# Reordering the opening of a two-block transformer kernel: activations first, query from unshifted activations

## What is computed

```
mod = silu(c) @ w_ada + b_ada                 # 1024 x 6144: shift, scale, gate, twice
sh1, sc1, gt1, sh2, sc2, gt2 = split(mod, 6)
h = rmsnorm(x, g_mix) * (1 + sc1) + sh1       # per token norm, per feature scale and shift
proj = h @ w_in                               # q, k, v, o, gates, u
q = q * 128 ** -0.5
# gates -> log_sigmoid, cumulative sums and maxima over the tokens -> decay of an mLSTM,
# in both directions, four heads of 128; then pooling, output projection, feed forward, a second block
```

## Time and profile before

| | us |
|---|---|
| median of 3 runs | 1655.7 |
| lowest, highest | 1654.61, 1656.57 |
| the profiled execution, its own time | 1656.27 |
| its span, first to last instruction | 1654.5 |
| PE busy | 1631.2 (99% of the span) |
| DVE busy | 1072.2 (65%) |
| ACT busy | 737.4 (45%) |
| POOL busy | 237.6 (14%) |
| DMA | 199.3 MB, 120 GB/s over the span |

### The profile page before, as it was taken

One profiled execution on the slowest core, in us unless ns is written; L12 is line 12 of the kernel. 1 busy time (PEld: TensorE's weight loads), 2 busy tenths in 40 slices (PEclk: granted clock), 3 DMA queues, 4 the chain that ended last, 5 costly groups with the idle time before them and its releaser, 6 DMA issues.

```text
span 1654.5 us, 20244 instructions
## 1 busy us (share of the span) xinstructions
PE 1631.2 (99%) x7833; PEld 1308.0 (79%) x7833; DVE 1072.2 (65%) x1358; ACT 737.4 (45%) x971; POOL 237.6 (14%) x255
## 2 busy tenths in 40 slices
PE   6999999999999999999999999999999999999999
PEld 3887778888898887887666788886688888888887
DVE  2897778543575577786766855548768876642464
ACT  3543334322374235646775433538822464431242
POOL 0014300050220000001766000004600000000000
PEclk9999999999999999999999999999999999999999
DMA  9556423222222232225664222220032222222223
GB/s 378 197 205 255 161 77 102 89 90 102 103 102 102 88 142 81 103 76 202 211 221 156 77 102 74 100 98 27 2 128 96 83 102 103 99 82 100 102 102 102
DMA packets 31151, 199.30 MB, mean 120 GB/s; under 512 B 3504, under 2 KB 4008, under 8 KB 10832
## 3 DMA queue, kind: packets, MB, share of 16 engines
q1 hardware_dynamic: 27168, 171.63, 28.9%
q10 hardware_dynamic: 3888, 26.38, 4.0%
HBM read 193.60 MB, written 4.40 MB: 120 GB/s over the span
## 4 chain that ended last, share of the span: by engine, by line
PE 90%; DVE 6%; ACT 2%; DMA 1%; issue 1%; POOL 0%; SPq 0%; DVEq 0%; ACTq 0%; POOLq 0%
PE bank1to L1869 14%; PE bank1to L1871 14%; PE bank1to L1870 14%; PE bank L1869 13%; PE bank L1870 12%; PE bank L1871 12%; PE bank L2319 2%; PE bank1to L2435 2%; PE bank L2447 1%; PE bank L2461 1%; DVE w_lo L1016 1%; DMA x<-x_in 1%; DVE ada_sum L1152 1%; PE bank L2153 1%; PE bank L1977 1%
## 5 line engine op out<-in xcount | busy, mean ns | idle before, releaser
L477 ACT ACTIVATE w_hi<-raw 128x2048 fp32r<-128x2048 f32 (+1 forms) x133 | 247.4, 1860 | 312.9 <-DMA raw<-slabs 300.2
L1016 DVE TENSOR_TENSOR w_lo<-raw,w_hi 128x2048 fp32r<-128x2048 f32 (+1 forms) x125 | 291.6, 2333 | 100.3 <-ACT w_hi L477 96.8
L1869 PE MATMUL bank<-h,w_hi 128*128 128x512 f32 (+1 forms) x736 | 290.5, 395 | 0.9 <-ACT qa L477 0.7
L1870 PE MATMUL bank<-h,w_hi 128*128 128x512 f32 (+1 forms) x736 | 285.9, 388 | 0.0
L1871 PE MATMUL bank<-h,w_lo 128*128 128x512 f32 (+1 forms) x736 | 285.6, 388 | 0.0
L1869 PEld LDWEIGHTS bank<-h,w_hi 128*128 128x128 f32 x736 | 138.2, 188 | 35.5 <-issue 7.8
L1871 PEld LDWEIGHTS bank<-h,w_lo 128*128 128x128 f32 x736 | 138.2, 188 | 28.9
L1870 PEld LDWEIGHTS bank<-h,w_hi 128*128 128x128 f32 x736 | 138.3, 188 | 27.9 <-issue 1.0
L1869 PE MATMUL bank1to<-h,w_hi 128*128 128x512 f32 (+1 forms) x416 | 159.7, 384 | 0.0
L1871 PE MATMUL bank1to<-h,w_lo 128*128 128x512 f32 (+1 forms) x416 | 159.3, 383 | 0.0
L1870 PE MATMUL bank1to<-h,w_hi 128*128 128x512 f32 (+1 forms) x416 | 159.3, 383 | 0.0
(11 more groups left out here) (519 smaller groups left out, 2746.1 us busy)
## 6 DMA issues: line engine op xcount, KB each, us to landing
raw<-slabs SPq DMA_DIRECT2D x127, 1024.0 KB, 4.8
ada_chunk<-ada ACTq DMA_DIRECT2D x24, 1024.0 KB, 8.1
p<-sum_rows SPq DMA_DIRECT2D x32, 640.0 KB, 5.5
x<-x_in SPq DMA_DIRECT2D x4, 1024.0 KB, 8.5
p<-decay_rows SPq DMA_DIRECT2D x6, 640.0 KB, 7.4
spill_x<-x SPq DMA_DIRECT2D x1, 2048.0 KB, 10.8
x<-spill_x SPq DMA_DIRECT2D x2, 1024.0 KB, 5.9
out<-x SPq DMA_DIRECT2D x8, 256.0 KB, 2.0
```

The costliest lines, as they stand in the source:

```text
L477: return act.activation(out, in_, f, **kw)
L1016: do.tell(dve.tensor_tensor(w_lo[:, n % SLOTS, part], raw[:, n % SLOTS, part], w_hi[:, n % SLOTS, part].bitcast(f32), ALU.subtract), "w_sp ...
L1869: pe.matmul(out, w[0], a[0], start=start, stop=False)
L1870: pe.matmul(out, w[0], a[1], start=False, stop=False)
```

## The change

- SP issues `cols`, the first half of `x`, `consts`, chunk pair 2, slab 0, then chunk pairs 3 to 7, `gw`, slab 1; slab 2 waits for chunk pair 7 (before: for chunk 6). ACT issues the second half of `x` and chunk pairs 0 and 1. A chunk pair is two blocks of 128 features by 1024 columns: pairs 0 to 3 hold the scale, 4 to 7 the shift.
- The norm's sum: ACT squares into a ring of four buffers, DVE adds the eight squares (seven additions), PE sums over the features with four matmuls of one column, ACT takes the root of 128x4, DVE inverts it, PE spreads it (`spread`) into bank 6, and DVE multiplies the tiles of `x` with it in place, four ahead of slab 0's tail and four in the loop.
- q_0 is computed from `x * gain` without the shift. Chunk pairs 4 to 7 are multiplied between its tiles, the shift's row is turned, and the shifted `h` is made in a second pass (DVE `tensor_scalar`, ACT rounded head, DVE tail). The gate product runs on it alone, with the product of the shift and q_0's weights (32 matmuls of two columns, `shift_product`) between its tiles; ACT adds that bias to q_0 as it empties the banks.
- The split of the gate weights moves from DVE to POOL. Fillers change in number and place. Several semaphores are merged under one name.

```diff
@@ sync
-            for k in range(0, KT, 4):
-                sp.dma_start(x[:, k:k + 4, :], x_d[:, k:k + 4, :]).then_inc(sem("x_in"), 16)
+            sp.dma_start(x[:, 0:4, :], x_d[:, 0:4, :]).then_inc(sem("x_in"), 16)
             sp.dma_start(consts[:], consts_d).then_inc(sem("consts_in"), 16)
-            sp.dma_start(gw[:], gate_w_d).then_inc(sem("consts_in"), 16)
+            first_ada(2)
...
                 if n == 1:
-                    sp.wait_ge(sem("ada_in6"), 16)
+                    for part in range(3, KT):
+                        first_ada(part)
+                    sp.dma_start(gw[:], gate_w_d).then_inc(sem("gate_w_in"), 16)
+                if n == 2:
+                    sp.wait_ge(sem("ada_in7"), 16)
@@ scalar
+            for k in range(KT):
+                if k >= 4:
+                    act.wait_ge(sem("sq_used"), max(1, k - 4))
+                do.tell(fn(squares_ring[k % 4], x[:, k, :], ACT.Square), "sq_ready", k + 1)
+            act.wait_ge(sem("first_total"), 2)
+            do.tell(fn(first_root, banks[7][:, 0:TOK], ACT.Sqrt, bias=eps), "root_ready", n_root)
             weight_head(0)
             mod_copy(0, banks[4])
+            for k in range(KT):
+                act.wait_ge(sem("h_scaled"), max(4, k + 1))
+                do.tell(fn(h_hi[:, k, :], x[:, k, :], ACT.Copy, scale=gain[:, k:k + 1]), "unshifted_head", k + 1)
+            weight_head(1)
+            mod_copy(1, banks[5])
+            act.wait_ge(sem("shift_split"), 1)
+            for k in range(KT):
+                ...
+                do.tell(fn(h_hi[:, k, :], x[:, k, :], ACT.Identity, scale=gain[:, k:k + 1], bias=mod[:, SH1 + k:SH1 + k + 1]),
+                        "h_head", k + 1)
             ada_refill(KT, KT + 2)
+            weight_head(2)
+            act.wait_ge(sem("shift_taken"), 1)
+            for t in range(2):
+                tile_ready("q_0", t)
+                free(fn(qk[:, t, :], banks[t][:], ACT.Identity, scale=DH ** -0.5, bias=shift_bias[:, t:t + 1]), "q_0", t)
+            act.wait_ge(sem("h_ready"), KT)
             ada_refill(KT + 2, KT + 4)
             act.wait_ge(sem("gates_done"), 1)
@@ vector
+            for k in range(4):
+                do(dve.tensor_tensor(x[:, k, :], x[:, k, :], root_bank[:], ALU.mult))
             weight_tail(0)
+            first_mod(0, SC1, banks[4])
+            ...
+            for k in range(KT):
+                if k < 4:
+                    do.tell(dve.tensor_tensor(x[:, k + 4, :], x[:, k + 4, :], root_bank[:], ALU.mult), "h_scaled", k + 5)
+                dve.wait_ge(sem("unshifted_head"), k + 1)
+                do.tell(dve.scalar_tensor_tensor(h_lo[:, k, :], ...), "unshifted_ready", k + 1)
+            weight_tail(1)
+            first_mod(1, SH1, banks[5])
+            ...
+            shifted(0)
+            for k in range(KT):
+                if k + 1 < KT:
+                    shifted(k + 1)
+                dve.wait_ge(sem("h_head"), k + 1)
+                do.tell(dve.tensor_tensor(h_lo[:, k, :], (t0, t1)[k % 2][:], ...), "h_ready", k + 1)
+            dve.wait_ge(sem("shift_done"), 1)
+            ...
+            weight_tail(2)
             do(dve.memset(row_parts[:].bitcast(f32), 0.0))
-            for n in range(1, 3):
-                weight_tail(n)
@@ tensor
+            mod_chunk(0)
+            kept_busy(banks[3], 12)
+            pe.wait_ge(sem("first_total"), 1)
+            for t in range(TOK):
+                last = pe.matmul(banks[7][:, t:t + 1], rs[:, P * t:P * t + P], mean[:, 0:1], start=True, stop=True)
+            last.then_inc(sem("first_total"), 1)
+            mod_chunk(1)
+            kept_busy(banks[3], 5)
+            pe.wait_ge(sem("consts_in"), 16)
+            pe.wait_ge(sem("first_total"), 3)
+            spread(first_root, "first_total")
+            mod_chunk(2)
+            kept_busy(banks[3], 8)
+            mod_chunk(3)
+            kept_busy(banks[3], 2)
             mod_turn(0, banks[4])
+            kept_busy(banks[3], 16)
             pe.wait_ge(sem("w_split"), 1)
             for k in range(KT):
+                pe.wait_ge(sem("unshifted_ready"), k + 1)
                 ...
+                for n in {2: (4, 5), 4: (6,), 5: (7,)}.get(k, ()):
+                    mod_chunk(n)
+                if k == 6:
+                    mod_turn(1, banks[5])
+            pe.wait_ge(sem("gate_w_split"), 1)
+            for k in range(KT):
+                shift_product(k, SLAB0["q_0"], banks[7], 1)
+                pe.wait_ge(sem("h_ready"), k + 1)
+                gates = three(banks[5][:], (gw_hi[:, k, :], gw_lo[:, k, :]), (h_hi[:, k, :], h_lo[:, k, :]), k == 0, k == KT - 1)
+            gates.then_inc(sem("gates_done"), 1)
```

More of the change, by code:

```diff
@@ L574, in root_copy @@
                 do.tell(fn(rs[:], root_bank[:], ACT.Copy), "root_copied", n)
-            def norm():
-                squares([x[:, k, :] for k in range(KT)], sq)
-                root(rs)
             def heads(stage, shift=None, place=h_hi, between=None):
@@ new lines, in _ @@
+            for k in range(2, KT):
+                dve.wait_ge(sem("sq_ready"), k + 1)
+                ins = dve.tensor_tensor(total, total, squares_ring[k % 4], ALU.add)
+                if k < KT - 1:
+                    do.tell(ins, "sq_used", k)
+                else:
+                    do.tell(ins, "first_total", 1)
+            n_root = 1
+            dve.wait_ge(sem("root_ready"), n_root)
+            do.tell(dve.reciprocal(first_root, first_root), "first_total", 3)
+            dve.wait_ge(sem("first_total"), 4)
@@ L1219, in _ @@
+            do.tell(dve.tensor_scalar(shift_bias[:], shift_bias[:], DH ** -0.5, None, ALU.mult), "shift_taken", 1)
+            weight_tail(2)
             do(dve.memset(row_parts[:].bitcast(f32), 0.0))
-            for n in range(1, 3):
-                weight_tail(n)
             do(dve.tensor_scalar(half_gain[:], cols[:, COLS["g_head"]:COLS["g_head"] + H1], 0.5, None, ALU.mult))
@@ L1864, in _ @@
         def _(pe):
-            n_sq = 0
             def three(out, w, a, start, stop):
```

248 lines of the change are left out of this document (119 added, 129 removed).

## The result

The changed kernel is slower: a median of 1660.0 us (15 runs, 1657.7 to 1663.8) against 1655.2 (15 runs, 1654.3 to 1657.4), a ratio of 1.0030 with a 95% interval from 1.0022 to 1.0038. Forecast were 1656.0 us and a range up to 1659.5. Even among the rest single executions differ by more than the effect of some parts, so both kernels were profiled twice.

The account below looks back on a forecast made before the run. PE was taken as the bound, busy 1631.2 of 1654.5 us. Of 9.8 us won at the product 9.5 go by k_0; decay work 2.55 later puts `weighted` at +0.3: 1655.7 + 0.3 = 1656.0, range 1651.5 to 1659.5 (8 in 10).

Parts of the forecast that it names:

- the sum from the first product to the transposes of the decay rows: PE from product at 31.3 to k_0 at 57.2, then 28.0 us plus 0.5 waiting for q_1's tail: transposes at 85.8.
- Up to the product: Opening: column total at 18.5 us, held 2.1 by fillers; first product at 31.3 against 41.14, 9.8 won.
- From the product to k_0: PE's chunks, turn and second pass between product and k_0: 9.5 of 9.8 us given back, k_0 at 57.2 against 57.55.
- the step that decides: Decay work after late gate rows: DVE starts at 60.8 against 58.25, 2.55 later; `weighted` at 92.75 against 92.45, +0.3 us.
- From here both lists are as before: Behind `weighted`: the lists stay as before, after a delay of +0.3 us.
- Rival 3: Slower: PE at 1.2 GHz when the product starts, 2.7 us there and as much in fillers before: 1661; chance 0.07.
- Rival 1: Faster: opening fillers cost nothing, column total at 16.4, product at 27.9, all behind 3.4 us earlier: 1652.0; chance 0.22.
- Rival 2: Slower: SP's lone queue after 17 us delays slab 1 and the shift, at 250 GB/s by 6.5 us: 1662; chance 0.05.
- POOL's split: POOL splits `gw` beside DVE's tails 3 to 7; DVE lines up to 1.80 us, at most 0.3 us shows.
- The base: Profiled execution 1656.27 us, 0.6 above the median of the runs; forecast counted from 1655.7.

Follow-up runs that it names:

- the kernel before with a late decay: Seven more memsets of a row on DVE ahead of the first softplus step, against the kernel before; median 1659.3 us.
- the tuned one-pass kernel: One of four variants of the kernel before: x first, all eight chunks before the product, shift in one pass; medians 1656.4, 1655.1, 1655.8, 1655.5 us.

## Why the prediction was wrong

The step that failed is the sum from the first product to the transposes of the decay rows. Its terms were the right ones, and they were short: 25.9 us to k_0 where 27.41 were measured, and 0.5 us of waiting for slab 3's tail where 1.03 were. With the 0.5 us by which the product itself came late this puts `weighted` 2.7 us behind the kernel before, where I had said 0.3. On top came a term that I had put at nothing: I priced PE's wait in front of the second pass by its length alone, and behind it the clock fell in many executions.

**Up to the product: right.** Pair 0 landed at 12.33 (12.4), x at 10.0 (9.9), the additions ended at 16.5 (16.4), the fillers held the column total until 18.94 (18.5), and from it to the product passed 12.89 us (12.8). The product came at 31.83 (31.3); 0.4 of the 0.5 is the chunk and the fillers behind it, of which 18 and not 16 ran at half pace, and 0.15 of that is a slip of the sum (1.7, 3.6 and 0.95 make 6.25, not 6.1).

**From the product to k_0: the terms right, three sizes short.** Forecast 25.9 us, measured 27.41. The stretch from the product to the shift's bias being ready took 15.67 instead of 15.1 (+0.57): each return from a chunk to the product costs (the first matmul 0.50 instead of 0.39, and 0.33 to the next instead of 0.23, at 37.97). The second pass took 10.47 instead of 9.95 (+0.52): 1.31 us a tile, not 1.24, with 0.55 for the `tensor_scalar` of two column operands against 0.49. From the last tail to k_0 passed 1.27 instead of 0.85 (+0.42). With the product's 0.5 that is k_0 at 59.24 instead of 57.2: 2.0 of the 2.4 us by which `weighted` missed. Each term was taken from a row of the nearest form in a stretch without interruptions; all erred to the same side. One reading of the sum was wrong too: it called 4.9 us a time in which PE waits for the second pass. Of what was measured there 3.8 us are PE's own 32 shift matmuls, and only 2.15 go when the pass is left out.

**The decay work: the right place, and 2.2 us late.** I called the late gate rows "the step that decides" and priced the transposes by DVE and PE about alike (85.6 and 85.8; the second is 57.2 + 28.0 + 0.5 = 85.7). They came out alike, and both late: the decay rows ready at 87.89, PE there at 88.22. Softplus started at 62.97 (60.8), 2.0 of the 2.2 by k_0's delay, and from it to the rows passed 24.9 us (24.8). What decides is k_0: 1.7 to 1.85 of the 2.7 to 3.0 us. The late decay work adds the 1.0 to 1.1, through slab 3's tail, which stands in the middle of DVE's list and for which I had 0.5 us; and had the tail not held PE, the decay rows would have, for 0.7 us (estimate above). Both have to come earlier, as in the run that moved the tail; there the 1.0 were gone. PE's arrival at the transposes sets `weighted`, 6.95 or 6.96 us later in every profile.

**"From here both lists are as before": right** for the order of the work (3.0 at `weighted`, 3.1 at the end, in the second profiles), with a chance of 1.3 us more by a late decay row.

**Rival 3 had the mechanism and the wrong place.** I looked for a low clock at the start of the product and found the fillers to leave no gap. The gap is the 1.1 us in front of the second pass, which I had counted as a wait of PE and not followed further. In 10 of 23 executions the clock was low for some 12 to 18 us, by their mean clock, and these took 3.4 us more (1662.5 against 1659.1). The 13 others have their median at 1659.1 and the kernel with the wait filled at 1659.25, inside my range if barely; with the falls it is 1660.0, outside. Rival 1's fillers may be worth up to 2.0 us in the fastest executions, which no profile caught; on the median of 14 they were worth 1.2. Rival 2 did not happen: slab 1 and the shift were never waited for (and its 6.5 us would be 6.8: 7.9 / 0.25 less 24.8). POOL's split ran beside DVE's tails, and the price there was higher than my row of 1.80: two of the subtractions took 1.41 and 2.76 us instead of 0.75, so that the last five took 6.57 in a row. PE never waited for one: at most 0.3, as said.

```profile
34.71 6.57 DVE L1255 SCALAR_TENSOR_TENSOR h<-x,gain,h 128x512 fp32r<-128x512 f32 x5
```

**The base.** 1656.27 stood 1.3 us above the next profile of the same kernel. The sum against the median was right to take, but the 0.4 us in it that lay ahead of the product were part of the 9.8 that I took for won.

So the account, in the second profiles: 9.2 won; 5.1 given back to four chunks and a turn inside the product (16.01 us to its end, less 48 x 0.2275), 3.8 to the 32 shift matmuls between the gates (what is left of 11.40 us to k_0 without the gates' 24 x 0.2275 and the next term), 2.15 to PE's waiting for the second pass (shown by leaving it out), 1.1 to the late decay work through slab 3's tail (shown by moving the tail and the decay rows together): 3.0 lost. On top come 0.75 to 1.6 by the clock, shown by the fillers and counted in two ways. What the first count leaves open is no more than single executions differ by, such as the 1.3 us of the late decay row.

## What to carry to other kernels

Splitting a dependent step to start its first half earlier pays only for what the split itself does not put on the engine that is full: here PE got 8.9 us more to do between the same two points and won 9.2. When a stage's gain is followed to the next meeting point, ask which instruction there is reached last, and look for producers (a weight tail) that stand in the middle of a list which the change delays. Where two things come within 0.3 us of each other, as the decay rows and PE do here, moving the later one alone gains no more than that. The wait of a microsecond on TensorE had two prices here, its length and the chance that the clock falls behind it; fill such a wait with matmuls that nobody reads, in the wait and not beside it.

## What the runs showed of the hardware

- TensorE's granted clock fell to half in the second pass, 1.2 and 1.6 us behind a wait of 1.1 us, for 17.1 us, in the two profiles with fewer fillers; by the mean clock the same happened in 10 of 23 executions of the changed kernel, and it did not in its two profiles, though the wait is the same. Behind a wait of 2.26 us (the kernel before with a late decay) it fell for 3.4 us. It also fell for 3.4 us at 1131.7 us in one profile of the kernel before and not in the other. With eight more matmuls of 128x128 in the wait of 1.1 us none of 11 executions fell there, nor any of 11 of the kernel made from it.
- When the clock first rose varied: 24 fillers took 3.61 to 5.06 us in seven profiles, and with 8 in their place PE stood at 1.2 GHz until 24.3 and 24.8 us.
- A DVE instruction on 128x8 numbers took 1.73 us instead of 0.17 beside a POOL subtraction, and of DVE's subtractions of 128x512 beside POOL's split two took 1.41 and 2.76 us instead of 0.75. POOL's masks of 128x256 took between 0.41 and 2.34 us; what ran beside the long ones was not tested.
- Behind the last DMA issue of the output the span went on for 2.4 us in one profile and 3.2 in another (the tuned one-pass kernel's). No run explains it.
